# A list of expert units with fewer loads, slot lists in fp32r, and down panels with two neighbouring rows on each partition

## The reference

```python
logits = (xt @ router_w + router_b).astype(f32)
top_val, top_idx = lax.top_k(logits, TOP_K)            # 4 of 32 experts
gate = jax.nn.softmax(top_val, axis=-1)
...
gu = xblk @ w_gu[e] + b_gu[e]                          # 1024 -> 2048
g, up = gu[:, :D_FF], gu[:, D_FF:]
g = jnp.minimum(g, SWIGLU_LIMIT)
up = jnp.clip(up, -SWIGLU_LIMIT, SWIGLU_LIMIT)
act = (up + 1.0) * (g * jax.nn.sigmoid(SWIGLU_ALPHA * g))
return act @ w_down[e] + b_down[e]                     # 1024 -> 1024
...
out = jnp.zeros((N + 1, D_), f32).at[tok_buf].add(yb.astype(f32) * w_buf[:, None])[:N]
```

## Time and profile before

| | |
|---|---|
| median of 3 runs | 2966.05 us |
| the profiled execution | 2965.58 us |
| its span, first to last instruction | 2963.8 us |
| TensorE busy in the span | 2843.9 us (96%) |
| VectorE, ScalarE, GpSimd busy | 1032.1, 536.3, 187.5 us |
| moved by DMA | 584.59 MB |
| mean granted TensorE clock | 0.975 of full speed |

### The profile page before, as it was taken

How to read it: one execution, slowest core, us unless ns; L and a number is a source line. 1 busy time by engine, 2 the same in 40 slices (tenths; PEclk the granted TensorE clock), 3 DMA queues, 4 the chain that set the end, 5 groups by cost and what they waited for, 6 DMA issues and landing times.

```text
span 2963.8 us, 34847 instructions
## 1 busy us (share of the span) xinstructions
PE 2843.9 (96%) x14311; PEld 1395.7 (47%) x14312; DVE 1032.1 (35%) x1907; ACT 536.3 (18%) x1024; POOL 187.5 (6%) x282
## 2 busy tenths in 40 slices
PE   7999899999999999999969999998999999999999
PEld 3555544554444444444445545545545444444444
DVE  5941432333333333333253357244133222212101
ACT  3313310100001010001042233323133201000000
POOL 3210200000000000000000024000000000000000
PEclk9999899999999999999979999999999999999999
DMA  7256589999999999999963100200200141221310
GB/s 235 64 175 225 194 336 367 393 396 350 382 379 383 372 374 381 381 380 372 391 224 142 57 1 29 79 29 29 72 29 15 57 156 57 85 76 38 106 50 29
DMA packets 197405, 584.59 MB, mean 197 GB/s; under 512 B 15133, under 2 KB 23812, under 8 KB 197220
## 3 DMA queue, kind: packets, MB, share of 16 engines
q1 hardware_dynamic: 191744, 567.25, 50.8%
q0 software_dynamic: 4736, 14.88, 1.7%
q10 hardware_dynamic: 772, 0.26, 0.0%
HBM read 576.06 MB, written 4.19 MB: 196 GB/s over the span
## 4 chain that ended last, share of the span: by engine, by line
PE 89%; DVE 7%; ACT 1%; issue 1%; DMA 1%; SPq 0%; DVEq 0%; ACTq 0%; PEldq 0%
PE psum_all L213 86%; PE psum_all L221 3%; DVE scratch L1293 1%; DMA panels<-in_ada_w 1%; DVE scratch L3945 1%; DVE scratch L1350 1%; DVE hidden L2603 1%; SPq L190 0%; DVE panels L1293 0%; DVE resid L1755 0%; DVE scratch L1362 0%; DVE scratch L3344 0%; DVE panels L1350 0%; ACT hidden L458 0%; DVE hidden L1751 0%
## 5 line engine op out<-in xcount | busy, mean ns | idle before, releaser
L213 PE MATMUL psum_all<-panels,scratch 128*64 128x512 f32 (+4 forms) x6104 | 921.2, 479 | 4.8 <-issue 2.4
L213 PE MATMUL psum_all<-hidden,panels 128*128 128x512 f32 (+1 forms) x1792 | 788.3, 601 | 9.0 <-ACT hidden L458 8.7
L213 PEld LDWEIGHTS psum_all<-panels,scratch 128*64 128x64 f32 (+2 forms) x6104 | 363.8, 130 | 498.9 <-issue 432.8
L213 PEld LDWEIGHTS psum_all<-hidden,panels 128*128 128x128 f32 (+1 forms) x1792 | 333.2, 191 | 417.5 <-issue 402.4
L213 PE MATMUL psum_all<-scratch,panels 128*128 128x512 f32 (+2 forms) x816 | 306.8, 538 | 4.7 <-DVEq L4124 1.7
L213 PEld LDWEIGHTS psum_all<-scratch,panels 128*128 128x128 f32 (+1 forms) x816 | 152.1, 188 | 161.3 <-issue 149.4
L2603 DVE TENSOR_TENSOR hidden<-hidden,psum_all 128x512 f32<-128x512 f32 x264 | 164.4, 681 | 71.3 <-PE psum_all L213 70.9
L213 PE MATMUL psum_all<-scratch 128*64 128x128 f32 (+9 forms) x1284 | 161.9, 351 | 22.3 <-DVEq L3963 8.5
L213 PEld LDWEIGHTS psum_all<-scratch 128*64 128x64 f32 (+3 forms) x1284 | 109.0, 167 | 84.8 <-issue 60.5
L221 PE MATMUL psum_all<-const,scratch 128*128 128x128 f32 (+4 forms) x887 | 122.5, 269 | 17.9 <-DMA scratch<-in_c_ctx 7.7
L2311 ACT ACTIVATE scratch<-psum_all 128x512 f32<-128x512 f32 (+1 forms) x49 | 25.8, 527 | 602.0 <-PE psum_all L221 602.0
(11 more groups left out here) (356 smaller groups left out, 2085.4 us busy)
## 6 DMA issues: line engine op xcount, KB each, us to landing
panels<-in_exp_w_gu SPq DMA_DIRECT2D x132, 2048.0 KB, 13.4
panels<-in_exp_w_down SPq DMA_DIRECT2D x66, 2048.0 KB, 12.1
panels<-in_w_in SPq DMA_DIRECT2D x17, 2048.0 KB, 10.4
panels<-in_w_mod SPq DMA_DIRECT2D x11, 2048.0 KB, 8.2
panels<-in_ada_w SPq DMA_DIRECT2D x14, 1024.0 KB, 7.3
panels<-in_ada_w SPq DMA_DIRECT2D x5, 2048.0 KB, 20.8
panels<-in_ffn_w_gate SPq DMA_DIRECT2D x5, 2048.0 KB, 7.6
panels<-in_ffn_w_up SPq DMA_DIRECT2D x5, 2048.0 KB, 7.7
```

The source lines that it names most:

```text
L213: ins = self.pe.matmul(out, lhsT, rhs, start=start, stop=stop)
```

## The change

It has three parts.

1. The list of units is new. Unit 0 (expert 0) has 64 slots, ranks 25 and 26 have 32, and unit 2 uses the panels that unit 1 has loaded, since both are rank 0: unit 1 (`HOLDS`) hands no slot back, unit 2 (`SHARES`) waits for no load and hands them back. So 192 panels are loaded, where it was 198.
2. The slot lists are made in fp32r. The gates are split into three fp32r numbers whose sum is the fp32 gate (`dve_thirds`), the token number is the fourth column, and VectorE sums the three parts. The shares of a 96-slot unit come four tiles at a time, so that their last 32 slots fill four strips of rows.
3. A down panel puts two neighbouring rows on each partition, one packet of 8192 bytes. The transposes of the activations pick every second column, so that the features meet their rows.

```diff
-    large = [(NE - 1, 0, 96), (0, 0, S)] + [(r, 0, S if r < 4 else 96) for r in range(1, 15)]
...
+    units = [(NE - 1, 0, HALF), (0, S, HALF), (0, 0, S), (25, 0, QUARTER), (26, 0, QUARTER)]
...
-        dst = self.slots[s][:, 0:k * cols].rearrange("p (k c) -> p k c", k=k)
-        sp.dma_start(dst, src.rearrange("(k p) c -> p k c", p=P)).then_inc(self.loaded[s], 16)
+        dst = self.slots[s][:, 0:k * cols].rearrange("p (g c) -> p g c", g=k // rows_each)
+        sp.dma_start(dst, src.rearrange("(g p e) c -> p g (e c)", p=P, e=rows_each)).then_inc(self.loaded[s], 16)
...
-            sels = [sel[:, u % 2, :, :], sel_last][:2 if UNITS[u][2] == 96 else 1]
+            sels = [sel_r[:, u % 2, :, :], sel_last][:2 if UNITS[u][2] == 96 else 1]
             for i, slots_at in enumerate(sels):
                 for t in range(TT):
-                    vals = gate_0[:, t, :] if u == 0 else gate_r[:, t, r:NE + 1:NE - r]
-                    ins = mm(bank[:, 2 * i:2 * i + 2], slots_at[:, t, :], vals, t == 0, t == TT - 1)
+                    vals = gate_0[:, t, :] if u == 0 else gate_r[:, t, r, :]
+                    ins = mm(bank[:, 4 * i:4 * i + 4], slots_at[:, t, :], vals, t == 0, t == TT - 1)
...
+        def dve_thirds(dve, step, dst, src, rest):
+
+            c = [dst[:, :, :, i] if len(dst.shape) == 4 else dst[:, :, i] for i in range(3)]
+            dve.tensor_copy(c[0], src).then_inc(dve_done, 1)
+            dve.wait_ge(dve_done, step.next())
+            dve.tensor_tensor(rest, src, c[0].bitcast(F32), ALU.subtract).then_inc(dve_done, 1)
+            dve.wait_ge(dve_done, step.next())
+            dve.tensor_copy(c[1], rest).then_inc(dve_done, 1)
+            dve.wait_ge(dve_done, step.next())
+            dve.tensor_tensor(c[2], rest, c[1].bitcast(F32), ALU.subtract).then_inc(dve_done, 1)
+            dve.wait_ge(dve_done, step.next())
...
-                dve.tensor_copy(slot_tok[:, u:u + 1], bank[:, 1:2])
-                dve.tensor_copy(slot_vals[:, u, 0:2], bank[:, 0:2]).then_inc(banks.free, 1)
+                dve.tensor_copy(slot_tok[:, u:u + 1], bank[:, 3:4])
+                dve.tensor_copy(slot_vals[:, u, 1:2], bank[:, 3:4])
+                dve.tensor_reduce(slot_vals[:, u, 0:1], bank[:, 0:3], AX_X, ALU.add).then_inc(banks.free, 1)
...
-                ins = mm.transpose(bank[:, b * P:(b + 1) * P], ub[:, i * 512 + b * P:i * 512 + (b + 1) * P], ident)
+                first = i * 512 + b // ROWS_EACH * ROWS_EACH * P + b % ROWS_EACH
+                ins = mm.transpose(bank[:, b * P:(b + 1) * P], ub[:, first:first + ROWS_EACH * P - 1:ROWS_EACH], ident)
...
-                    if n == HALF and k == 3:
+                    if n == HALF and k == 3 and u != HOLDS:
                         ins.then_inc(panels.used[s], 1)
...
+            if UNITS[u][2] == 96:
+                if i % 4:
+                    return
+                nos = [y_fill(u, chunks(u) + i + j) for j in range(4)]
+                pe.wait_ge(shares_free, nos[3])
+                for m in range(2):
+                    f = slice((2 * m + i // 4) * P, (2 * m + i // 4 + 1) * P)
+                    for ys in (y_hi, y_lo):
+                        for h, no in zip(halves, nos[2 * m:2 * m + 2]):
+                            mm(moe_y(no)[:, :], ys[h, f], tokens_r[h, 0, :], ys is y_hi, False)
+                f = slice(512 + i // 4 * P, 512 + (i // 4 + 1) * P)
+                strips = [(slice(q * QUARTER, (q + 1) * QUARTER), no) for q, no in zip((0, 2, 1, 3), nos)]
+                for h, no in strips:
+                    mm(moe_y(no)[:, :], y_hi[h, f], tokens_r[h, 1, :], False, False)
+                for h, no in strips:
+                    mm(moe_y(no)[:, :], y_lo[h, f], tokens_r[h, 1, :], False, True).then_inc(shares_full, 1)
+                return
...
+            into(gu(e1, 0))
+            down(e0)
+            into(gu(e1, 1))
+            panels.at_load += 2
+            down(e1)
+            panels.at_load += 2
+            into(gu(e3, 0))
+            panels.at_load += 2
+            into(gu(e3, 1))
+            into(gu(e4, 0))
+            down(e3)
+            into(gu(e4, 1))
```

More of the change, by code:

```diff
@@ L2343, in pe_expert_in @@
             if n == QUARTER:
-                pe_quarter_in(pe, mm, u, bias, [pe_rows_panel(pe) for _ in range(2)], 0)
+                pe_quarter_in(pe, mm, u, bias, [pe_rows_panel(pe, u) for _ in range(2)], 0)
                 mid()
@@ L2438, in pe_expert_out @@
                 pe_quarter_out(pe, mm, u, pair, t, no)
-            mm.done(panels.used[pair[1][0]])
+            if u != HOLDS:
+                mm.done(panels.used[pair[1][0]])
         def share_tile(u, i):
@@ L2619, in sp_moe, with into, down @@
         def sp_moe(sp):
-            def into(w):
+            def into(w, rows_each=1):
                 for p in range(2):
-                    panels.load(sp, w[p * 512:(p + 1) * 512, :])
+                    panels.load(sp, w[p * 512:(p + 1) * 512, :], rows_each)
+            def down(e):
+                into(expert_dram(a["exp_w_down"], e), ROWS_EACH)
             def gu(e, which):
```

110 lines of the change are left out of this document (56 added, 54 removed).

## The result

The changed kernel took 2900.64 us, the median of 4 runs (2899.1 to 2902.26), against 2966.49 (2965.52 to 2968.39) beside it: a ratio of 0.9777, 95% interval 0.976 to 0.9794. Predicted were 2892.0, with a range of 2880 to 2912; the narrower range of the forecast itself, 2884 to 2900, was just missed. So 65.9 us went where 73.4 were forecast. The profiled execution took 2901.15 us, of which 2899.5 are span.

What follows compares the result with a forecast made beforehand. TensorE's work, not panel transfers, was taken to bound the expert stage. 37.0 + 18.5 + 18.9 + 3.0 − 4.0 = 73.4 us off 2965.6 gave 2892.2, predicted 2892; range 2880 to 2912, narrower 2884 to 2900.

Steps and rivals of the forecast that it cites:

- The bound: Expert stage: TensorE's work sets the time and paces the panel transfers, leaving 7.2 and 3.5 us of cover per turn.
- The new list of units: Expert stage: two units shrink from 64 to 32 slots, unit 0 from 96 to 64; 37.0 us less TensorE work.
- Slot lists in fp32r: Each unit's slot-list matmuls: half the records go, 0.44 us in each of 42 groups, 18.5 us saved.
- Shares of the 96-slot units: Results back to tokens in eleven units: each half takes 1.79 us instead of 2.65, 18.9 us saved.
- Start: Stage opening: one token-transpose round, half of unit 1's list and a VectorE wait go; 3.0 us earlier.
- Joins: Waits for VectorE's additions: 2.7 us at unit 3's shares, 1.3 at the stage's end, together 4.0 us lost.
- Held slots: Unit 2 on unit 1's panels: four panels land by 22.2 us, needed at 23.6; 0 taken, upper bound 10.2 us.
- Strided transposes: Activation transposes reading every second column, 158 records: 0 taken, +12.6 us if the stride doubled each.
- Large packets: Sixty-four down panels in 8192-byte packets: transfers lie wholly under TensorE's cover, so worth 0.
- the one of held slots or strided transposes: Rival in the expert stage: these cost 10.2 or 12.6 us, giving 2902 to 2905; chance 0.15.
- 369 GB/s as a ceiling: Rival: panel transfers become the stage's bound at their usual pace, stage ends at 1455, total 2926; chance 0.06.
- slow large packets: Rival: down panels take 9.8 us each at 13.4 GB/s per engine, total 3115, slower than before; chance 0.03.

Runs made afterwards that it cites:

- list_only: Changed kernel with unit 2's own panels, one-row down panels, fp32 slot lists and 96-slot shares two tiles at a time; 2934.0 us, ratio 0.9885 to the kernel before.
- own_panels: Changed kernel with unit 2 loading its own six panels again and unit 1 handing its slots back; 2902.2 us, ratio 0.9782 to the kernel before.
- plain_turns: Changed kernel with activation transposes reading neighbouring columns, 8192-byte packets kept, result wrong but work equal; 2899.5 us, ratio 0.9776 to the kernel before.
- lists_fp32: Changed kernel with the slot lists' operands in fp32 again, same four columns; 2931.5 us, ratio 0.9885 to the kernel before.
- late_x: Changed kernel with token transposes moved between the two down panels, and some 32-slot units' first activation transposes between their gate panels; 2900.7 us.
- best_two: Changed kernel with opened and late_x together, and shares two tiles at a time for the two 96-slot units before a 32-slot one; 2895.4 us, ratio 0.9758.
- opened: Changed kernel with unit 4 made a 64-slot unit (rank 24) and rank 26's 32-slot unit moved to unit 30; 2899.3 us, ratio 0.9768.

## Why the prediction was right, and where it was off

The mechanism was right: TensorE's records set the time of the stage, and what shortened them came through for the most part. Two of its signs of being wrong did show: a gap before a panel of unit 4, and activation transposes that are longer than with neighbouring columns. By its own steps:

- **The bound** held. SyncE's queue waited 882.1 us for TensorE in 184 waits. Only the opening has one wait the other way.
- **The new list of units**, with its share of start and joins 37.0 − 4.0 + 1.1 = 34.1 us: 33.2 measured by list_only, with a wait of 4.4 us for a panel and 4.7 us of half clock in it that the prediction did not have. Without these, and without 2.2 us of other waits, its stage would be 39.4 us shorter, where 37.0 were worked out.
- **Slot lists in fp32r**, 18.5 us: each list lost the predicted 0.44, but the whole gave about 13. The step that failed is "What counts is therefore every TensorE record in the stage", applied to records that hide a latency. The prediction looked for cover on VectorE (33% busy) and not on ScalarE, whose copy of the turned activations must be through before the one bank of transposes can be filled again. In the kernel before, the slow list covered it. After it, 20 waits of 0.2 to 0.8 us take 8.1 us instead of 2.9.
- **Shares of the 96-slot units**, 18.9: the turn gives 1.70 for 1.72. One wait of 2.56 us at the end of the stage comes off, since the four free banks were looked at only where a 64-slot unit follows: about 16 in the stage, 12 to 15 in the whole time.
- **Start**, −3.0: the first strips came at 374.92 us instead of 379.86 in the two profiles (4.9 earlier), but over the thirteen profiles of changed kernels they came at 373.0 to 380.6. From the first slot list to the first strips it is 18.32 us at a granted clock of 0.50 before and 13.47 at 0.63 after, so a part of the 4.9 is the clock. That the three terms came is seen (list of unit 1 to token transposes 1.12 us instead of 2.19, for one); their size is not shown.

```profile
361.54:379.86 18.32, 14.04 (x56) 9.87 (x56) 8.39 (x33) 5.75 (x13) 4.00 (x11) 0.50 0.46 164
```

```profile
361.45:374.92 13.47, 8.64 (x41) 5.05 (x39) 8.38 (x34) 5.39 (x11) 3.53 (x7) 0.63 0.32 99
```

- **Joins**, +4.0: waits for VectorE went from 4.5 to 8.2 us, +3.7. That the size fits is luck: 2.56 of it are those of the shares, named above. The list alone brings 1.2 (5.7 us in list_only): the 2.56 at unit 3's shares that were forecast as 2.7, while the waits at the end of the stage went down and not up by 1.3.
- **Held slots**, 0 with a fit of 22.2 against 23.6 us: the fit was named as the tightest place and failed, by 4.8 us. TensorE was ready at 497.3 us, 22.7 behind the first free slot (474.6), nearly as worked out. The fourth panel was there at 502.1, 27.5 behind it. What was wrong is the 5.1 us per panel: it came from the best 15 us of the earlier trace rows, with an empty queue assumed at time 0, while the panel before was still landing until 477.6 us. By the windows the core moved 375 and 380 GB/s from 482 to 502, 5.5 to 5.6 us per panel. That it was put down to the held slots was wrong too, as own_panels shows.

```profile
482.00:492.00 10.00, 10.00 (x123) 6.22 (x116) 6.66 (x12) 0.00 (x0) 0.00 (x0) 1.00 0.95 375
492.00:502.00 10.00, 5.10 (x76) 3.19 (x75) 1.69 (x6) 1.87 (x4) 1.69 (x5) 1.00 1.02 380
```

- **Strided transposes**, 0 with a bound of 12.6: 2 to 4 us. The bound was read too low: 0.08 us is that of a token transpose of 64 slots, while four activation transposes take 0.59 us in plain_turns, so that doubling all 158 would have cost 23 us. **Large packets**, 0: right for this kernel.
- **The clock** was no term. It took 9.0 us in the stage instead of 7.0; lists_fp32 shows that it could have been 24.

Added up over the stage, with the waits for VectorE taken once, under the joins, 70.4 us were forecast and 57.7 came: 4.8 for the panel, 5.2 for ScalarE, 2 to 4 for the transposes, 2.0 for the clock make 14 to 16 of the missing 12.7; against that stands the list's own gain, 2.4 us larger than worked out, which no row here explains. The start gave 1.9 more than forecast, and the part behind the stage 1.5, of which no row shows the cause; the clock there varies by as much between kernels. The turns say the same in small. Predicted were 65.3 and 63.9 us; 65.85 and 64.45 came. Of the 0.55 in the first, 0.22 is the named wait for ScalarE and 0.13 the transposes; 0.2 belongs to the estimate of lists and shares. In the second, 0.44 is ScalarE, and 0.17 the transposes.

So part of the forecast's nearness is errors that offset each other. Of the rivals, the one of held slots or strided transposes (2902 to 2905) came nearest to what was missing, though with less than half of each price, and its wait did not come from the held slots. That of 369 GB/s as a ceiling is refuted by 397 over the stage, that of slow large packets by the median landing of a down panel (14.8 us, against 15.4 for the others, whose packets have 4096 bytes).

## What to carry to other kernels

A record that is made shorter gives its time only until the next thing on that engine needs another one: before a term is written down as count times saving, look at what stood behind the shortened work and which copy, on which engine, it gave time to. A transfer's fit is to be worked out with a queue that is still full and the rate of an ordinary stretch, not the best one, and two short units in a row were its worst case here. When waits of the compute engine go, test the size of transfers again: a change that was worth nothing here came to be worth some 3 us. And take the clock of each trace apart before a gain of a few us is put down to a change: in late_x and best_two half or more of what the stage gained was half clock.

## What the runs showed of the hardware that was not expected

- The granted clock fell to 0.5 for 3.4 us in turn after turn of otherwise full work (lists_fp32, six turns of 96 and 64 slots, 1.7 us each), in a kernel whose turn is 1 us longer than the changed kernel's; list_only, with a turn 2.5 us longer, has it in two. The cause is open.
- Stretches at 0.5 stood right behind waits of TensorE: at 502.2 us behind 4.80 us in the changed kernel, at 1360.2 behind 2.57 in opened, at 1404.2 behind 2.96 in best_two. At the first and the last of these, 64 records took 5.35 us, which take 3.66 at full clock.
- fp32 transposes whose stationary operand is read at a step of two take 0.68 us for four, against 0.59, and their weight loads 192 ns on average against 141.
- The core held 397 GB/s over 1058 us (own_panels), and 410 over the turn of 128 and 32 slots (changed kernel).
